# Turning the pages of a paged latent cache by DMA transposes of 16-bit planes

## What is computed

```python
def page_block(phys):
    kn, kr, v = mla_keys(cache_l[phys], w_uk, w_uv, k_norm_nope)   # kn = rms_norm((c @ w_uk) per head)
    return partial_softmax(mla_scores(qn, qr, kn, kr), v)

m_p, l_p, a_p = lax.map(page_block, page_table.T)
```

## Time and profile before

| | us |
|---|---|
| runs | 1597.24, 1595.16, 1598.21 (median 1597.24) |
| the profiled execution's own time | 1594.3 |
| its span, first to last instruction | 1592.2 |
| PE busy (98% of the span) | 1553.5 |
| DVE busy (47%) | 750.8 |
| ACT busy (48%) | 770.2 |
| POOL busy (13%) | 202.2 |
| first to last page transpose (L1794) | 124.4 to 1225.8 |
| HBM read and written | 132.62 MB and 6.74 MB |

### The profile page before, as it was taken

The page is one execution under the profiler, slowest core; times in us unless marked ns, Lnnn a source line. Parts: engine busy times, 40 slices in busy tenths (PEclk is TensorE's granted clock), DMA queues, the critical chain, the costliest instruction groups (busy, mean ns, idle before and its releaser), DMA issues.

```text
span 1592.2 us, 27599 instructions
## 1 busy us (share of the span) xinstructions
PE 1553.5 (98%) x9804; PEld 1285.1 (81%) x9804; DVE 750.8 (47%) x1512; ACT 770.2 (48%) x2793; POOL 202.2 (13%) x104
## 2 busy tenths in 40 slices
PE   6899999999999999999999999999999999999998
PEld 5776777877877878878788787787777899999998
DVE  5854333545344543444443444534213465877643
ACT  2334556565445564454654546444656334344331
POOL 0000201211111111211111111121121100000000
PEclk9999999999999999999999999999999999999999
DMA  8421012421123311124211231111412456555551
GB/s 257 141 78 43 16 31 57 112 71 39 47 57 94 84 31 31 34 81 113 62 32 31 62 97 31 31 31 49 124 31 83 144 171 216 179 157 173 181 185 54
DMA packets 130338, 140.90 MB, mean 88 GB/s; under 512 B 32352, under 2 KB 78976, under 8 KB 130072
## 3 DMA queue, kind: packets, MB, share of 16 engines
q1 hardware_dynamic: 125606, 137.15, 29.0%
q10 hardware_dynamic: 4602, 2.06, 0.6%
HBM read 132.62 MB, written 6.74 MB: 88 GB/s over the span
## 4 chain that ended last, share of the span: by engine, by line
PE 92%; DVE 4%; ACT 2%; ACTq 1%; issue 1%; DVEq 0%
PE ps L1803 15%; PE ps L1805 14%; PE ps L1804 14%; PE ps L2210 5%; PE ps L2211 5%; PE ps L2212 5%; PE ps L1794 4%; PE ps L1824 2%; PE ps L1842 2%; PE ps L1895 2%; PE ps L2158 2%; PE ps L2159 1%; PE ps L2160 1%; PE ps L1896 1%; PE ps L1897 1%; PE ps L1961 1%
## 5 line engine op out<-in xcount | busy, mean ns | idle before, releaser
L719 ACT ACTIVATE ksq<-ps 128x128 f32<-128x128 f32 x1024 | 268.3, 276 | 424.5 <-PE ps L1805 424.5
L1803 PE MATMUL ps<-ukh,cTh 128*128 128x512 f32 x1024 | 418.6, 409 | 0.1
L1805 PE MATMUL ps<-ukh,cTl 128*128 128x512 f32 x1024 | 402.1, 393 | 0.0
L1804 PE MATMUL ps<-ukl,cTh 128*128 128x512 f32 x1024 | 400.6, 391 | 0.0
L621 POOL TENSOR_TENSOR rk<-kss,mhalf 128x32 f32<-128x32 f32 x32 | 177.7, 5552 | 550.9 <-DVE kss L1496 550.9
L1803 PEld LDWEIGHTS ps<-ukh,cTh 128*128 128x128 f32 x1024 | 193.0, 188 | 52.5 <-issue 14.6
L1805 PEld LDWEIGHTS ps<-ukh,cTl 128*128 128x128 f32 x1024 | 192.5, 188 | 42.7
L1804 PEld LDWEIGHTS ps<-ukl,cTh 128*128 128x128 f32 x1024 | 193.4, 189 | 34.6
L719 ACT ACTIVATION_READ_ACCUMULATOR ksq<-ps 128x1 f32 x1024 | 211.3, 206 | 0.0
L906 ACT ACTIVATE wh<-wraw 128x2048 fp32r<-128x2048 f32 x44 | 84.3, 1915 | 134.1 <-PE ps L2212 126.2
L1500 DVE TENSOR_TENSOR wl<-wraw,wh 128x2048 fp32r<-128x2048 f32 x44 | 100.8, 2290 | 76.2 <-ACT wh L906 76.0
(11 more groups left out here) (480 smaller groups left out, 2794.4 us busy)
## 6 DMA issues: line engine op xcount, KB each, us to landing
clat<-cache_mla SPq DMA_DIRECT2D x128, 256.0 KB, 2.6
wraw<-w_in SPq DMA_DIRECT2D x16, 1024.0 KB, 5.1
wraw<-w_up SPq DMA_DIRECT2D x16, 1024.0 KB, 5.4
wraw<-w_down SPq DMA_DIRECT2D x16, 1024.0 KB, 5.0
braw<-w_in SPq DMA_DIRECT2D x24, 512.0 KB, 3.8
crope<-cache_mla SPq DMA_DIRECT2D x128, 32.0 KB, 2.4
sst<-state_gdn SPq DMA_DIRECT2D x32, 128.0 KB, 3.4
gdn_sample<-sst SPq DMA_DIRECT2D x32, 128.0 KB, 2.2
```

The lines of the kernel that those rows point to most:

```text
L719: i = nc.scalar.activation(ksq[:, half_, P * h:P * h + P], ps[:, k % 3, P * h:P * h + P], ACT.Square, accum_out=kss[:, n // 4 % 2, n % 4, ...
L1803: mm(out, cTh[:, n % 2, c], ukh[:, c, cols], start=c == 0, stop=False)
L1804: mm(out, cTh[:, n % 2, c], ukl[:, c, cols], start=False, stop=False)
L1805: i = mm(out, cTl[:, n % 2, c], ukh[:, c, cols], start=False, stop=c == 3)
```

## The change

PE no longer transposes the pages. Each page of `clat` is read as 1024 numbers of 16 bits per token. POOL (`split_planes`) copies the low halves and the high halves apart into `planes` (128 x 1024 of 16 bits, one buffer). SP (`turn`) issues a DMA that transposes `planes` as eight 128 x 128 blocks of 16 bits into `turned` (two buffers). DVE (`join_planes`) interleaves the two halves again, into `cTr`. ACT's copy out of PSUM (L707 before) goes; ACT's `turned_page` starts with the rounding to `cTh`.

The waits: `split_planes(n)` waits for page n and for transpose n - 1 (`tr_landed`). `turn(n)` waits for `planes_ready` n and for join n - 2 (`ct_raw`). `join_planes(n)` waits for `tr_landed`, and at n % 4 == 0 for `qk_done`. Pages now land on a semaphore per ring slot. POOL's `group` is split into `means` (behind the split of page 4g + 6) and `group` (behind that of page 4g + 7). `ksq`, which takes ACT's squares, goes from two buffers to one, `olat` and `onew` overlie other tiles, and one load of weights moves from slot 28 to slot 34.

```diff
--- before.py
+++ after.py
@@ -14,6 +14,7 @@
+U16 = mybir.dt.uint16
@@ -285,7 +286,9 @@
         wuvf, e = place("wuvf", [P, 4, D], F32, taken["cTr"][0])
         assert e == o
         rpT, o = place("rpT", [P, 2 * P], F32, o)
-        ksq, o = place("ksq", [P, 2, 512], F32, o)
+        ksq, o = place("ksq", [P, 512], F32, o)
+        planes, o = place("planes", [P, 512], F32, o)
+        turned, o = place("turned", [P, 2, 512], F32, o)
         pst, o = place("pst", [P, 2, 4, 32], F32, o)
         kss, o = place("kss", [P, 2, 4, H], F32, o)
         rk, o = place("rk", [P, 2, 4, H], F32, o)
@@ -300,8 +303,8 @@
         alpha, o = place("alpha", [P, 2, H], F32, o)
         asel, o = place("asel", [P, 1 + H], F32, o)
         gate, o = place("gate", [1, 1], F32, o)
-        olat, o = place("olat", [P, NS, 4, H], F32, o)
-        onew, o = place("onew", [P, NS, 4, H], F32, o)
+        olat, _ = place("olat", [P, NS, 4, H], F32, taken["prows"][0])
+        onew, _ = place("onew", [P, NS, 4, H], F32, taken["rpT"][0])
         oseq, _ = place("oseq", [P, 4, H, NS], F32, taken["onew"][0])
 
         TOP = 212800
@@ -419,8 +422,7 @@
             return ukl[:, :, (n - UK) * 512:(n - UK + 1) * 512] if n in (UK, UK + 1) else wl[:, n % 2]
 
 
-        B_TR, B_SCORE, B_SUM, B_PAIR, B_ROWS = 3, 4, 4, 5, 7
-        trp = ps[:, B_TR, :].rearrange("p (c n) -> p c n", c=4)
+        B_SCORE, B_SUM, B_PAIR, B_ROWS = 4, 4, 5, 7
         stp = ps[:, B_SCORE, :].rearrange("p (t n) -> p t n", t=4)
         pvt = ps[:, B_SUM, :].rearrange("p (c n) -> p c n", c=4)
 
@@ -471,11 +473,18 @@
             def page(u, n):
                 pg = sp.value_load(ptab[0:1, bass.ds(n, 1)] if not isinstance(n, int) else ptab[0:1, n:n + 1], min_val=0, max_val=I["cache_mla"].shape[1] - 1)
                 rows_ = I["cache_mla"][0][bass.ds(pg, 1), :, :].rearrange("o p n -> p (o n)")
-                sp.dma_start(clat[:, u, :], rows_[:, 0:LAT]).then_inc(S(f"pages_landed{u // 4}"), 16)
-                sp.dma_start(crope[:, u, :], rows_[:, LAT:LW]).then_inc(S(f"pages_landed{u // 4}"), 16)
+                sp.dma_start(clat[:, u, :], rows_[:, 0:LAT]).then_inc(S(f"page_landed{u}"), 16)
+                sp.dma_start(crope[:, u, :], rows_[:, LAT:LW]).then_inc(S(f"page_landed{u}"), 16)
+
+            def turn(n):
+                sp.wait_ge(S("planes_ready"), n + 1)
+                wait(sp, "ct_raw", n - 1)
+                sp.dma_start(turned[:, n % 2].bitcast(U16).rearrange("p (x n) -> p x n", n=P), planes[:].bitcast(U16), transpose=True).then_inc(S("tr_landed"), 16)
 
             for u in range(8):
                 page(u, u)
+            turn(0)
+            turn(1)
             sp.wait_ge(S("ukT_act"), H // 2)
             sp.wait_ge(S("ukT_dve"), H // 2)
             for n in range(8, RING):
@@ -541,9 +550,11 @@
                 if i == F_END - 1:
                     sp.wait_ge(S("rows_out"), 48)
                     sp.wait_ge(S("a_read"), a_count(f"pv{H - 1}"))
-                    for jj in range(3):
+                    for jj in range(2):
                         pair_weights(jj)
                     pair_rows_in(0)
+                if i == B_START - 1:
+                    pair_weights(2)
 
             sp.dma_start(O["conv_sample"][0, :, 0:CONVW - 2, :], I["state_conv"][0, :, 1:CONVW - 1, :]).then_inc(S("conv_shift"), 16)
             for i in range(2 * NT):
@@ -552,6 +563,8 @@
                     sp.wait_ge(S("pv_used"), i // 8 - 1)
                     for m in range(n, n + 4):
                         page(m % RING, m)
+                if i % 2 == 1 and i // 2 + 2 < NT:
+                    turn(i // 2 + 2)
                 front_loads(i)
                 b, k = pair_slot(i)
                 if b is not None:
@@ -616,15 +629,29 @@
             nc.gpsimd.memset(mhalf[:], -0.5).then_inc(S("att_clear"), 1)
             g.wait_ge(S("att_clear"), 2)
 
-            def group(gg, y):
+            def means(gg, y):
                 g.wait_ge(S("ms_ready"), gg + 1)
                 nc.gpsimd.tensor_tensor(rk[:, y], kss[:, y], mhalf[:], ALU.pow).then_inc(S("rk_ready"), 1)
+
+            def group(gg, y):
                 g.wait_ge(S("s_ready"), gg + 1)
                 nc.gpsimd.tensor_tensor(gate[:], mhalf[0:1, 0, 0:1], mhalf[0:1, 0, 0:1], ALU.add)
                 nc.gpsimd.partition_all_reduce(smax[:].rearrange("p t h -> p (t h)"), ssc[:, y].rearrange("p t h -> p (t h)"), P, RMAX).then_inc(S("smax_ready"), 1)
 
-            for gg in range(NG):
-                group(gg, gg % 2)
+            def split_planes(n):
+                g.wait_ge(S(f"page_landed{n % RING}"), 32 * (n // RING) + 32)
+                wait(g, "tr_landed", 16 * n)
+                nc.gpsimd.tensor_copy(planes[:].bitcast(U16).rearrange("p (x l) -> p x l", x=2), clat[:, n % RING, :].bitcast(U16).rearrange("p (l x) -> p x l", x=2)).then_inc(S("planes_ready"), 1)
+
+            for n in range(3):
+                split_planes(n)
+            for n in range(3, NT + 4):
+                if n < NT:
+                    split_planes(n)
+                if n % 4 == 2 and n >= 6:
+                    means(n // 4 - 1, (n // 4 - 1) % 2)
+                if n % 4 == 3 and n >= 7:
+                    group(n // 4 - 1, (n // 4 - 1) % 2)
 
         @block.scalar
         def _(act):
@@ -701,10 +728,6 @@
                 nc.scalar.activation(ukT[h], ps[:, 4 + h % 4, :], ACT.Copy).then_inc(S("ukT_act"), 1)
 
             def turned_page(n):
-                act.wait_ge(S("tr_done"), n + 1)
-                if n % 4 == 0:
-                    wait(act, "qk_done", n // 4)
-                nc.scalar.activation(cTr[:, :, tokens(n)], trp, ACT.Copy).then_inc(S("ct_raw"), 1)
                 act.wait_ge(S("ct_raw"), n + 1)
                 wait(act, "half_done", 2 * (n - 1))
                 nc.scalar.activation(cTh[:, n % 2], cTr[:, :, tokens(n)], ACT.Copy).then_inc(S("ct_hi"), 1)
@@ -714,9 +737,9 @@
                 act.wait_ge(S("half_done"), k + 1)
                 if half_ == 0 and n % 4 == 0:
                     wait(act, "rk_ready", n // 4 - 1)
-                wait(act, "ksq_ready", k - 1)
+                wait(act, "ksq_ready", k)
                 for h in range(4):
-                    i = nc.scalar.activation(ksq[:, half_, P * h:P * h + P], ps[:, k % 3, P * h:P * h + P], ACT.Square, accum_out=kss[:, n // 4 % 2, n % 4, 4 * half_ + h:4 * half_ + h + 1])
+                    i = nc.scalar.activation(ksq[:, P * h:P * h + P], ps[:, k % 3, P * h:P * h + P], ACT.Square, accum_out=kss[:, n // 4 % 2, n % 4, 4 * half_ + h:4 * half_ + h + 1])
                 i.then_inc(S("ksq_ready"), 1)
 
             def turned_rope(gg):
@@ -1066,6 +1089,12 @@
 
 
             v.wait_ge(S("att_clear"), 2)
+
+            def join_planes(n):
+                v.wait_ge(S("tr_landed"), 16 * n + 16)
+                if n % 4 == 0:
+                    wait(v, "qk_done", n // 4)
+                V.tensor_copy(cTr[:, :, tokens(n)].bitcast(U16).rearrange("p c (t x) -> p x c t", x=2), turned[:, n % 2].bitcast(U16).rearrange("p (x c t) -> p x c t", x=2, c=4)).then_inc(S("ct_raw"), 1)
 
             def split_lo(n):
                 v.wait_ge(S("ct_hi"), n + 1)
@@ -1471,9 +1500,12 @@
                 elif i == 2 * NT - 5:
                     z_low(1)
 
+            join_planes(0)
             split_lo(0)
             for n in range(NT):
                 g, t = n // 4, n % 4
+                if n + 1 < NT:
+                    join_planes(n + 1)
                 beside(2 * n)
                 if n + 1 < NT:
                     split_lo(n + 1)
@@ -1787,13 +1819,6 @@
                 i.then_inc(S("ukT_done"), 1)
             pe.wait_ge(S("acc_read"), KC + 32)
 
-            def transposes(n):
-                pe.wait_ge(S(f"pages_landed{n // 4 % 3}"), 128 * (n // RING) + 128)
-                wait(pe, "ct_raw", n)
-                for c in range(4):
-                    k = nc.tensor.transpose(trp[:, c, :], clat[:, n % RING, P * c:P * c + P], ident)
-                k.then_inc(S("tr_done"), 1)
-
             def keys(n, half_):
                 k, cols = 2 * n + half_, slice(512 * half_, 512 * half_ + 512)
                 out = ps[:, k % 3, :]
@@ -1806,6 +1831,8 @@
                 i.then_inc(S("half_done"), 1)
 
             def rope_columns(gg):
+                for u in range(4 * gg, 4 * gg + 4):
+                    pe.wait_ge(S(f"page_landed{u % RING}"), 32 * (u // RING) + 32)
                 wait(pe, "acc_done", gg - 1)
                 wait(pe, "accT_ready", (gg - 1) // 4)
                 wait(pe, "s_parts", gg)
@@ -2121,13 +2148,10 @@
                 if b is not None:
                     pair_pe(b, k)
 
-            transposes(0)
             for n in range(NT):
                 g, t = n // 4, n % 4
                 if t == 3:
                     query_products(g)
-                if n + 1 < NT:
-                    transposes(n + 1)
                 if t == 0 and g >= 1:
                     score_columns(g - 1)
```

## The result

The changed kernel takes 1610.03 us (median of 4 runs, 1608.13 to 1615.73); the kernel before took 1597.72 us (4 runs, 1595.16 to 1599.36) beside it. The ratio is 1.0092, 95% interval 1.0077 to 1.0106: slower by 0.9%, 12 us. The profiled execution's own time is 1608.13 us, its span 1606.3 us.

What follows compares the result with a forecast made beforehand. PE, busy 98% of the span, was taken as the bound. -60 + 36 + 12 + 36 = +24 us on 1594.3 gave 1618, written as 1620 us in the median's terms; range over the cases 1552 to 1765.

Steps and rivals of the forecast that it cites:

- quick-turn rival: DMA transpose of a page takes only 2.6 to 4 us: 1557 us, between 1550 and 1590; chance 0.36.
- Removed, -60: PE's page transposes: 0.47 us for each of 128 pages, 60 us won (56 to 68).
- Split 1.6 and join 1.2 us: Added per page: POOL's split 1.6 us (0.9 to 2.2), DVE's join 1.2 us (0.7 if two at once).
- The turn, 5 us: The transposing DMA per page, taken as 5 us, with 2.6 and 7.9 as ends.
- (a): Page 4g + 3's turn, issued behind four page loads, delays DVE, ACT and PE: 24 x 1.5 = 36 us.
- the sign that I had named: PE idle before U_'s user at page 4g + 2's second slot, put down to ACT or DVE, 1.5 us in 24 groups.
- (c): Joins and roundings standing ahead of a chain in a slot: 1.5 us in 24 groups, 36 us.
- (b): One planes buffer: split n + 1 waits for transpose n; 12 us lost in the last four groups.
- the GpSimd loop binds: POOL's serial round, 35.7 us with a reload before the power, exceeds PE's group time: +40 us, 1660; chance 0.15.
- the start: The start of the loop gains and loses within 2 us.
- the granted clock: Clock row at the top in every slice, so PE's speed was taken as not in question.
- VectorE beside GpSimd: DVE held up by POOL's longer occupation: nothing added, as L1073 took 0.68 us inside POOL's power.

Runs made afterwards that it cites:

- the untransposed kernel: Changed kernel without the split and the turn; DVE's join copies the page as it is, so the transposition is left out: 1544.97 us, ratio 0.9677.
- the late join: Changed kernel with DVE's join, split_lo and ACT's turned_page moved behind the side work of the slot's first half: 1595.04 us, ratio 0.9994.
- section 8: Changed kernel with two planes buffers, one page load ahead of page 4g+3's turn, join behind side work: 1563.99 us; another, early join, power replaced by a copy: 1558.27 us.

## Why the prediction was right, and where it was not

The forecast was 1620 us and slower; it is 1610 and slower. That it came so near is luck in part: with the turn as it was measured, the prediction's own terms give the 1557 us of its quick-turn rival. It took 9 us too much off, its losses were 84 us where 65 were measured, and a turn taken too long stood in for costs that it had put at nothing.

- **Removed, -60.** Measured as 51 us by the untransposed kernel, which still pays for its joins. The spacing of starts came nearer than the changed kernel's 34 us less of TensorE's busy time, which holds what low clock and broken streams added; in the untransposed kernel the busy time fell by 54.8.
- **Split 1.6 and join 1.2 us.** 1.18 and 0.78. The join was near my lower end (0.7), so 16-bit elements went at almost twice the rate per element of L1073.
- **The turn, 5 us.** The step that failed. It is 3.1 us, near the plain page load of the earlier trace rows and well under the 3.8 us row that I took as nearest. The Trainium skill's page "Advanced Engine Details and Errata", section X-Bar Transpose, pointed this way (by it 2.6), and the trace comes close to it; "VectorE: DVE Perf Modes", section The three transpose paths, would have given 10.5 us by my estimate from its block figure, and the trace disagrees.
- **(a) Page 4g + 3 late: the place was right, the price was not.** 29 of 39 waits at a join are there. But my formula said that nothing is lost under a turn of 3.5 us, and so it should have been nothing. It was worked out in page 54 alone, and there it even holds: the join's wait is 3.68 us in that page, and TensorE has no idle time there. In others DVE waits 5.6 us with a GDN step behind. In pages 4g + 2 TensorE is idle for 10.4 us, not 36, and the sign that I had named, waits for `U_` of ACT, is in no row. (a) and (c) together were 72 us; the middle groups of the untransposed kernel are 30.3 us shorter, 21.5 of it TensorE's idle time (27.2 against 5.7), and the late join took 17.8. That (c), work queued behind a join or a rounding, was a cost in kind is what the late join shows.
- **(b) One buffer, 12 us in the last groups.** Measured 28 in the last 8 groups, and not by the buffer alone: 19.3 of it went when the power and both waits put down to issue went from GpSimd. By the term's own formula the buffer costs nothing at the measured times, 4 x (1.18 + 3.1 + 0.2) = 17.9 us against the 25.2 that PE needs; it cost as a part of GpSimd's round.
- **The rival "the GpSimd loop binds"** had this mechanism and its decisive doubt. The pause ahead of the power is real: 151.4 us in 21 powers, 7.2 each, where I had said 6.5 if it exists. With a turn of 3.1 us the rival's sum is 35.7 less two times 1.9 and less what the split saves (4 x 0.4), 30.3 us, and the round is 30.2. So it binds where a group comes in 25 us and not where it comes in 34.5: with the shorter turn its 24 x 1.2 is gone, and of its last groups 4 x 5.1 us are left.
- **The quick-turn rival** (2.6 to 4 us, 1557) named the right duration and the wrong time: it gave (a) at most 12 us, (b) nothing and (c) 10 to 20, where the sum of all losses was 65.
- **Not in the sum:** the start, 6.3 us, which I had within 2; and the granted clock, which I had said not to be in question. It is 0.94 over the stretch from 1090 us, in which TensorE stood idle for 18.2 of 170 us, and 0.94 again with the late join, where it idled 20.5; in the untransposed kernel, idle for 1.3 us there, it is 1.00. A mean of 0.94 is mostly the level of 2.4 GHz with some of the time at 1.2. What that costs by itself no run here separates; where GpSimd sets the pace it may be nothing. It has a bound: over the whole span the clock is 0.986 of 1606.3 us here and 0.997 of 1541.8 in the untransposed kernel, so what is missing from full speed is 22 and 5 us, and at most some 18 of the 65 us are the clock's own.
- **VectorE beside GpSimd, put at nothing.** The row that I went by shows it beside the power; beside a split it is otherwise, as the last section shows.

## To carry to other kernels

Take the duration of a new asynchronous step and then ask which in-order engine stands at its result, and what is queued behind: here moving three calls behind work that was ready was worth 15 us, while making the step earlier was worth 6 alone and, done crudely, cost 9. Price an edit in the stretch where each engine's slack is smallest as well as in the typical one; one sampled page told nothing of the last groups, nor of the slots with the longest wait. Edits that look small one by one (6, 15 and 6 us) can be worth 46 together. My reading is that each alone leaves the next wait in the same chain; no two of them were run as a pair, so which pair makes the difference is not shown.

## What the hardware showed that I had not expected

- A transposing DMA from SBUF to SBUF of 128 x 1024 16-bit numbers lands 3.1 us after its issue (3.1 at best, 6.0 at worst) and holds SP's queue for 1.24 us; a plain page load of the same 256 KB lands in 2.5 us, and its row on the queue is 0.33 us (a page's two loads together hold the queue for 1.6, by the distance of their starts).
- GpSimd and VectorE hold each other up here, other than the row that I relied on. The split takes 1.04 us at the median and up to 2.17, the join 0.75 at the median and up to 1.42. A split and the join that starts inside it:

```profile
1021.55 1.04 POOL L644 COPY planes<-clat 128x1024 uint16<-128x1024 uint16 x1 [3.26 <-DMA turned<-planes]
1021.78 1.42 DVE L1097 COPY cTr<-turned 128x1024 uint16<-128x1024 uint16 x1 [2.77 <-PE ps L1854]
```

The one that starts first keeps its usual time; the second takes what is left of the first and nearly its own time on top. The join of 1021.78 starts 0.81 us before the split's end and takes 1.42; others start 0.48 and 0.66 us before it (523.92, 773.92) and take 1.10 and 1.27. The split of 1156.01 above starts 0.66 us before the end of a join (1155.91, 0.76 us) and takes 1.55. The 128 x 1024 rounding of weights at 742.52 starts 0.99 us before the end of a split (741.98, 1.53 us) and takes 2.08, where 1.22 is its median. So the second behaves as if it waited for the whole of the first, within its recorded duration. The Trainium skill, "SBUF — State Buffer", section Who interferes with whom, has one of the two wait for the whole of the other's instruction. For the splits the trace agrees with it. For the power it does not: in the kernel before, 28 subtractions L1073 lie wholly inside a power of 5.5 us and take 0.67 to 0.74 us each, as in the earlier trace rows.

In the changed kernel DVE's rows that meet a split are together some 35 us longer than the medians of their lines, and the splits 19 us longer than theirs (worked out from the timelines). How much of that reaches TensorE no run separates; it may be a part of (c) and of the 13 us left over in section 8.
